# Attention with sinks on Trainium2: a reordering of the fourth unit's scores, the last queries' copies, the squares and the exponentials

## The chip, the cores and the metric

The kernel runs on one core of one Trainium2 chip. The metric is the device time of one execution in microseconds, lower is better; where a kernel was run several times, the median is given.

## The reference, cut to what matters

The program computes two transformer blocks of two layers each over 256 tokens of width 1024, in float32. The change lies in one step of the second block's second layer: attention with 16 query heads and 4 key heads of 64, a window of 128 keys, and a learned sink logit per head.

```python
def banded_sink_attention(q, k, v, sinks):
    ...
    logits = jnp.einsum('bnqhgd,bnkhd->bnhgqk', qb, kw) * (dh ** -0.5)
    ...
    logits = jnp.where(valid[None, :, None, None], logits, -jnp.inf)
    m = jnp.maximum(jnp.max(logits, axis=-1), sink)
    probs = jnp.exp(logits - m[..., None])
    denom = jnp.sum(probs, axis=-1) + jnp.exp(sink - m)
    out = jnp.einsum('bnhgqk,bnkhd->bnhgqd', probs, vw) / denom[..., None]

def swa_sink_mixer(h, positions, w_qkv, q_norm, k_norm, sinks, w_out):
    qkv = h @ w_qkv
    ...
    q = apply_rope_2(rms_norm_2(q, q_norm), cos, sin)
    k = apply_rope_2(rms_norm_2(k, k_norm), cos, sin)
    o = banded_sink_attention(q, k, v, sinks)
    return o.astype(h.dtype) @ w_out
```

## The kernel before, in words

**Weights.** Every weight matrix is loaded in pieces of 1 MB (queue of SyncE), and each piece is cut into two units. ScalarE copies a unit into a high part (`hi_to`, L383, about a microsecond), VectorE subtracts that from the raw data into a low part (`lo_to`, L391), and TensorE multiplies with three products for one (high by high, high by low, low by high). A unit's buffer comes free when TensorE is done with the unit six places before. `hi_to(main, n)` and `lo_to(main, n)` treat all units below n that are not yet treated. In this stage `U` is the first unit of the attention's weights: U to U+3 are the keys, U+4 to U+7 the first half of the queries, U+8 and U+9 the values, U+10 to U+13 the last queries, and U+14 to U+21 the output projection.

**The attention stage** runs from about 1940 to 2064 us. Each engine has its order written out by hand, in `pe_window`, `act_window` and `dve_window`, and semaphores join them. An engine works strictly down its own list: whatever stands behind a waiting instruction waits too. The steps are:

- `qk(n, c)` on TensorE projects a quarter of group n (2 the keys, 0 the first queries, 1 the last queries). Two quarters fill a bank of PSUM.
- `squares(n, i)` on ScalarE (L2467) squares a bank for the norm, `gained(n, i)` on VectorE (L2541) copies the same bank, times the norm's gain, into `QB`. It waits for the squares. These are the "copies" of the change's name.
- `sums(n)` on TensorE (L2318) sums the squares over each head with products that are 2 columns wide; it waits for both of the group's squares. `scales(n)` on VectorE (L2563 and the small operations behind it) makes the inverse roots.
- `rope(n)` on TensorE (L2326) rotates `QB`; `cosines(n)` and `sines(n)` on VectorE (L2546, L2552, L2556) finish the rotation.
- Scores come in eight units. Unit u belongs to key head u // 2 and to half u % 2 of the queries; the even ones see 128 keys, the odd ones 256. `logits(u)` on TensorE (L2363) makes them; `begin(u)` on VectorE is `masked(u)` (adds the mask, L2576 or L2579) and `maxima(u)` (L2589 to L2595; an even unit's `begin` takes the next even unit too). `soft(u)` on ScalarE (L2477, L2479) is the exponentials. `turned(u)` is the transposition on TensorE (L2378) and its copy out on ScalarE (L2485).
- `weigh(g, t)` on TensorE (L2393) multiplies by the values, `weighed(g, t)` on VectorE (L2608 to L2617) divides by the denominators, and `rows(g, t)` transposes the result back (L2402), and splits it into high and low parts (ScalarE L2489, VectorE L2625).
- `pe_project` multiplies by the output weights (L408 to L410), and does `logits(7)`, `turned(4)` and so on between its first four units.

"The fourth unit" of the change's name is unit 3. The values are copied out of PSUM by ScalarE at L2503, and `qk(1, 0)` needs the bank they leave. What the change touches are the lists in `pe_window` (L2427 to L2436), `act_window` (L2497 to L2520) and `dve_window` (L2652 to L2672).

Of the kernel before, what the change touches and what calls it, by code (L numbers as in the profile page):

```python
# [244 lines left out]
def program(nc, ctx, d, out, known, draft):  # L245
# [35 lines left out]
    main = Side(sig, "", all_loads(d), NS + NX)  # L281
# [34 lines left out]
    def bk(b):  # L316
        return PSM[:, b, :]
# [11 lines left out]
    def take(b):  # L329
        claim_bank(b)  # L330
        return bk(b)
# [43 lines left out]
    def hi_to(s, n, end=None):  # L375
        while s.hi_at < min(n, len(s.w.units) if end is None else end):
            i = s.hi_at
            m, h = s.w.units[i]
            if h == 0:
                A.wait_ge(*s.landed[s.w.loads[m][3]].of(m))  # L380
            if i >= NU:
                A.wait_ge(*s.pe.of(("unit", i - NU)))
            A.activation(unit(s, i)[0], raw_half(s, i), ACT.Copy).then_inc(*s.w_hi.tick(i))  # L383
            s.hi_at += 1

    def lo_to(s, n, end=None):
        while s.lo_at < min(n, len(s.w.units) if end is None else end):
            i = s.lo_at
            hi, lo = unit(s, i)
            V.wait_ge(*s.w_hi.of(i))  # L390
            V.tensor_tensor(lo, raw_half(s, i), hi.bitcast(F), SUB).then_inc(*s.w_lo.tick(i))  # L391
            s.lo_at += 1
# [1910 lines left out]
    def pe_window():  # L2303
# [9 lines left out]
        def sums(n):  # L2313
            ps = take(SS_BANK[n])
            T.wait_ge(*act.of(f"wi.sq{n}"))
            for t in range(2):
                for c in range(4):
                    x = T.matmul(ps[:, 8 * t + 2 * c:8 * t + 2 * c + 2], SQ[:, c, t * P:(t + 1) * P], C("bd2"), start=True, stop=True)  # L2318
            x.then_inc(*pe.tick(f"wi.ss{n}"))
            empties(SS_BANK[n], (dve, f"wi.ss{n}"))  # L2320
# [48 lines left out]
        def turned(u):  # L2369

            nb, banks, E = u % 2 + 1, PT_BANKS[u], WE[u % 4]
            for b in banks:
                take(b)
            T.wait_ge(*act.of(f"wi.e{u}"))
            for j in range(4):
                for kb in range(nb):
                    o = (j * nb + kb) * P
                    x = T.transpose(bk(banks[o // 512])[:, o % 512:o % 512 + P], E[:, j, kb * P:(kb + 1) * P], ident)  # L2378
            x.then_inc(*pe.tick(f"wi.T{u}"))
            for b in banks:  # L2380
                empties(b, (act, f"wi.pt{u}"))

        def weigh(g, t):

            b = AV_BANK[g][t]
            ps = take(b)
            T.wait_ge(*act.of("wi.v"))
            for i in range(2):
                u = 4 * g + 2 * i + t
                T.wait_ge(*act.of(f"wi.pt{u}"))  # L2390
                for j in range(4):
                    for kb in range(t + 1):
                        x = T.matmul(ps[:, 256 * i + 64 * j:256 * i + 64 * j + 64], WP[u % 4][:, j, kb * P:(kb + 1) * P],  # L2393
                                     WV[:, kb, (2 * g + i) * 64:(2 * g + i + 1) * 64], start=kb == 0, stop=kb == t)
            x.then_inc(*pe.tick(f"wi.av{g}{t}"))
            empties(b, (dve, f"wi.z{g}{t}"))
# [30 lines left out]
        turned(2)  # L2427
        qk(1, 3)
        turned(1)
        sums(1)  # L2430
        weigh(0, 0)
        rope(1)
        turned(3)
        weigh(0, 1)
        rows(0, 0)
        rows(0, 1)  # L2436
# [23 lines left out]
    def act_window():  # L2460
        U = un["wi.qk2a"][0]

        def squares(n, i):
            if n != 2:
                A.wait_ge(*pe.of(f"wi.ss{0 if n else 2}"))
            A.wait_ge(*pe.of(f"wi.qk{n}{i}"))
            A.activation(SQ[:, 2 * i:2 * i + 2, :], heads(bk(QK_BANKS[n][i]), 2), ACT.Square).then_inc(*act.tick(f"wi.sq{n}", f"wi.sq{n}{i}"))  # L2467

        def soft(u):
            nm, sm, sk, _ = soft_cols(u)  # L2470
            gr, t = u // 2, u % 2
            L = WE[u % 4]
            _, r, _, _ = win_scales(gr // 2)
            A.wait_ge(*dve.of(f"wi.m{u}"))
            for j in range(4):
                n = 8 * t + 4 * (gr % 2) + HEAD[j]
                A.activation(L[:, j, :], L[:, j, :], ACT.Exp, scale=r[:, n:n + 1], bias=nm[:, j:j + 1], accum_out=sm[:, j:j + 1]  # L2477
                             ).then_inc(*act.tick(f"wi.e{u}"))
            A.activation(sk, sk, ACT.Exp).then_inc(*act.tick(f"wi.e{u}"))  # L2479

        def turned(u):
            A.wait_ge(*pe.of(f"wi.T{u}"))
            w = 512 // (P * (u % 2 + 1))
            for i, b in enumerate(PT_BANKS[u]):
                A.activation(flat(WP[u % 4][:, w * i:w * i + w, :]), bk(b), ACT.Copy).then_inc(*act.tick(f"wi.pt{u}"))  # L2485

        def rows(g, t):
            A.wait_ge(*pe.of(f"wi.zT{g}{t}"))
            A.activation(XH[:, 4 * g:4 * g + 4, t * P:(t + 1) * P], heads(bk(WZ_BANK[g][t]), 4), ACT.Copy  # L2489
                         ).then_inc(*act.tick(f"wi.h{g}{t}"))  # L2490

        hi_to(main, U + 8)
        squares(2, 0)
        hi_to(main, U + 10)
        squares(2, 1)
        hi_to(main, U + 12)
        squares(0, 0)  # L2497
        hi_to(main, U + 14)
        squares(0, 1)
        hi_to(main, U + 16)  # L2500
        A.wait_ge(*pe.of("wi.v"))
        for t in range(2):
            A.activation(WV[:, t, :], bk(t)[:, 0:256], ACT.Copy, scale=RR[:, t:t + 1]).then_inc(*act.tick("wi.v"))  # L2503
        soft(0)
        soft(2)
        hi_to(main, U + 17)
        soft(1)
        squares(1, 0)
        turned(0)
        turned(2)  # L2510
        hi_to(main, U + 19)
        soft(3)
        squares(1, 1)
        turned(1)
        hi_to(main, U + 20)
        turned(3)
        rows(0, 0)
        rows(0, 1)
        soft(4)
        soft(6)  # L2520
        hi_to(main, U + 21)
        soft(5)
        turned(4)
        turned(6)
        hi_to(main, U + 22)
        soft(7)
        turned(5)
        hi_to(main, un["wi.o2"][0] + NU)
        turned(7)
        rows(1, 0)  # L2530
        rows(1, 1)

    def dve_window():
        U = un["wi.qk2a"][0]
        sn = S("sinks")

        def gained(n, i):
            if n != 2:
                V.wait_ge(*pe.of(f"wi.ro{0 if n else 2}"))
            V.wait_ge(*act.of(f"wi.sq{n}{i}"))  # L2540
            V.tensor_scalar(QB[:, 2 * i:2 * i + 2, :], heads(bk(QK_BANKS[n][i]), 2), S("akn") if n == 2 else S("aqn"), None, MUL  # L2541
                            ).then_inc(*dve.tick(f"wi.g{n}{i}"))
# [40 lines left out]
        def maxima(u):  # L2583
            nm, _, sk, x = soft_cols(u)
            gr, t, L = u // 2, u % 2, WE[u % 4]
            _, r, _, _ = win_scales(gr // 2)
            r4 = r[:, 8 * t + 4 * (gr % 2):8 * t + 4 * (gr % 2) + 4].rearrange("p (a b) -> p b a", a=2)
            V.wait_ge(*dve.of(f"wi.l{u}"))
            V.tensor_reduce(x, L, AX, MAX, negate=True).then_inc(*dve.tick())  # L2589
            V.wait_ge(*dve.last())  # L2590
            V.tensor_tensor(x.rearrange("p (b a) -> p b a", b=2), x.rearrange("p (b a) -> p b a", b=2), r4, MUL).then_inc(*dve.tick())
            V.wait_ge(*dve.last())
            V.tensor_tensor(nm, x, NSK[:, 4 * gr:4 * gr + 4], MIN).then_inc(*dve.tick())
            V.wait_ge(*dve.last())
            V.tensor_tensor(sk, nm, sn[:, 4 * gr:4 * gr + 4], ADD).then_inc(*dve.tick(f"wi.m{u}"))  # L2595

        def begin(u):
            masked(u)
            maxima(u)
            if u % 2 == 0:  # L2600
                maxima(u + 2)
# [20 lines left out]
        def rows(g, t):  # L2622
            V.wait_ge(*act.of(f"wi.h{g}{t}"))
            h = XH[:, 4 * g:4 * g + 4, t * P:(t + 1) * P]
            V.tensor_tensor(XL[:, 4 * g:4 * g + 4, t * P:(t + 1) * P], heads(bk(WZ_BANK[g][t]), 4), h.bitcast(F), SUB  # L2625
                            ).then_inc(*dve.tick(f"wi.x{g}{t}"))
# [25 lines left out]
        masked(1)  # L2652
        lo_to(main, U + 16)
        maxima(1)
        gained(1, 0)
        lo_to(main, U + 17)
        begin(3)
        lo_to(main, U + 18)
        gained(1, 1)
        cosines(1)  # L2660
        scales(1)
        weighed(0, 0)
        sines(1)
        lo_to(main, U + 19)
        weighed(0, 1)
        begin(4)
        rows(0, 0)
        rows(0, 1)
        masked(5)
        lo_to(main, U + 20)  # L2670
        maxima(5)
# [327 lines left out]
```

## Time and profile before

| | us |
|---|---|
| median of 3 runs | 2325.43 |
| lowest and highest | 2322.65, 2327.29 |
| the profiled execution's own time | 2323.32 |
| its span | 2321.5 |
| mean granted TensorE clock (share of full) | 0.962 |

The rows below come from the profiled execution, in microseconds from the start of its span. Busy time of TensorE is modelled and includes the pipeline, so the start of an instruction is the safer number. In a timeline a row shows the start, the duration, the engine, the line, the operation, what it writes and reads, how many, and in brackets the idle time of the engine before it and what ended that. The granted clock is given as a share of full: 1.00 is 2.4 GHz and 0.50 is 1.2 GHz.

### The profile page before, as it was taken

Reading aid. Unit: us, or ns where it says so; the run is one execution under the profiler, and the core shown is the slowest. Engines: PE = TensorE matmul, PEld = TensorE weight load, DVE = VectorE, ACT = ScalarE, POOL = GpSimd, SP = SyncE. Lnnn points to the kernel's source line nnn. Section 1 sums busy time; section 2 is a strip of 40 time slices with the busy share of each in tenths; the row PEclk is TensorE's granted clock in tenths of the full one; section 3 lists DMA queues with packets and bytes.
Section 4 is the critical chain, followed back from the end, with each engine's and each line's share of the span. In section 5 each row is a group of like instructions: output and inputs, shape, how many; then the busy total and the mean of one; then the engine's idle time right before and its main releaser. Section 6 shows DMA issues by size and latency. Waiting matters only on the chain.

```text
span 2321.5 us, 30709 instructions
## 1 busy us (share of the span) xinstructions
PE 2159.3 (93%) x12344; PEld 1892.9 (82%) x12344; DVE 1773.2 (76%) x2344; ACT 1394.2 (60%) x1845; POOL 45.1 (2%) x22
## 2 busy tenths in 40 slices
PE   7999999889999999999999999577789999789998
PEld 6889989778888888888888888366689988679996
DVE  4776666769999989899999999666676667666665
ACT  4544445558777777787777878444454454454444
POOL 0020001010000000000000000000000000000000
PEclk9999999989999999999999999788899999889999
DMA  8436544549999999999999999233245545135552
GB/s 281 141 129 207 193 139 153 208 174 379 349 377 357 359 351 356 356 361 364 345 371 350 368 339 371 85 113 105 91 161 184 182 133 180 55 100 191 182 180 97
DMA packets 280165, 546.62 MB, mean 235 GB/s; under 512 B 8524, under 2 KB 113616, under 8 KB 279888
## 3 DMA queue, kind: packets, MB, share of 16 engines
q1 hardware_dynamic: 276800, 535.33, 65.9%
q10 hardware_dynamic: 3040, 8.72, 1.1%
q8 instruction: 100, 1.64, 0.3%
q0 software_dynamic: 176, 0.53, 0.1%
q14 instruction: 49, 0.40, 0.1%
HBM read 543.49 MB, written 1.05 MB: 235 GB/s over the span
## 4 chain that ended last, share of the span: by engine, by line
PE 87%; DVE 8%; ACT 3%; DMA 1%; issue 1%; DVEq 0%; SPq 0%; ACTq 0%
PE psum L408 19%; PE psum L410 18%; PE psum L409 18%; PE psum L402 8%; PE psum L403 8%; PE psum L404 8%; DVE wl L391 2%; PE psum L1689 1%; PE psum L1709 1%; DMA raw<-in_w_in 1%; PE psum L1699 1%; ACT XT L444 1%; PE psum L2393 1%; DVE arena L2137 0%; PE psum L437 0%
## 5 line engine op out<-in xcount | busy, mean ns | idle before, releaser
L391 DVE TENSOR_TENSOR wl<-raw,wh 128x1024 fp32r<-128x1024 f32 x640 | 771.6, 1229 | 201.9 <-ACT wh L383 196.8
L383 ACT ACTIVATE wh<-raw 128x1024 fp32r<-128x1024 f32 x640 | 662.8, 1050 | 319.2 <-PE psum L404 149.6
L402 PE MATMUL psum<-xh,wh 128*128 128x256 f32 x1600 | 464.2, 290 | 26.6 <-DVE wl L391 18.9
L391 DVE TENSOR_TENSOR wl<-arena,wh 128x1024 fp32r<-128x1024 f32 x384 | 458.0, 1221 | 32.4 <-ACT wh L383 23.6
L408 PE MATMUL psum<-wh,xh 128*128 128x512 f32 (+1 forms) x1152 | 457.6, 397 | 19.9 <-DVE xl L428 10.4
L383 ACT ACTIVATE wh<-arena 128x1024 fp32r<-128x1024 f32 x384 | 404.5, 1062 | 94.5 <-PE psum L410 94.5
L403 PE MATMUL psum<-xl,wh 128*128 128x256 f32 x1600 | 460.4, 288 | 0.0
L404 PE MATMUL psum<-xh,wl 128*128 128x256 f32 x1600 | 459.9, 287 | 0.0
L410 PE MATMUL psum<-wh,xl 128*128 128x512 f32 (+1 forms) x1152 | 451.1, 392 | 0.0
L409 PE MATMUL psum<-wl,xh 128*128 128x512 f32 (+1 forms) x1152 | 450.9, 391 | 0.0
L402 PEld LDWEIGHTS psum<-xh,wh 128*128 128x128 f32 x1600 | 314.8, 197 | 33.8 <-DVE wl L391 14.5
L403 PEld LDWEIGHTS psum<-xl,wh 128*128 128x128 f32 x1600 | 315.1, 197 | 1.6 <-issue 0.5
L404 PEld LDWEIGHTS psum<-xh,wl 128*128 128x128 f32 x1600 | 314.7, 197 | 0.0
L408 PE MATMUL psum<-wh,yh 128*128 128x512 f32 x736 | 288.5, 392 | 2.4 <-DVE yl L1837 1.4
L409 PE MATMUL psum<-wl,yh 128*128 128x512 f32 x736 | 287.0, 390 | 0.0
L410 PE MATMUL psum<-wh,yl 128*128 128x512 f32 x736 | 286.7, 390 | 0.0
L408 PEld LDWEIGHTS psum<-wh,xh 128*128 128x128 f32 x1152 | 218.9, 190 | 66.3 <-DVE xl L428 10.6
L410 PEld LDWEIGHTS psum<-wh,xl 128*128 128x128 f32 x1152 | 218.6, 190 | 46.1
L409 PEld LDWEIGHTS psum<-wl,xh 128*128 128x128 f32 x1152 | 219.1, 190 | 43.3
L408 PEld LDWEIGHTS psum<-wh,yh 128*128 128x128 f32 x736 | 138.4, 188 | 30.3 <-DVE yl L1837 1.6
L410 PEld LDWEIGHTS psum<-wh,yl 128*128 128x128 f32 x736 | 138.2, 188 | 29.0
L409 PEld LDWEIGHTS psum<-wl,yh 128*128 128x128 f32 x736 | 138.4, 188 | 26.9
(362 smaller groups left out, 1633.2 us busy)
## 6 DMA issues: line engine op xcount, KB each, us to landing
arena<-in_moe_g SPq DMA_DIRECT2D x72, 1024.0 KB, 7.3
arena<-in_moe_u SPq DMA_DIRECT2D x72, 1024.0 KB, 7.8
raw<-in_moe_d SPq DMA_DIRECT2D x64, 1024.0 KB, 7.5
arena<-in_moe_d SPq DMA_DIRECT2D x48, 1024.0 KB, 6.9
raw<-in_ff_up SPq DMA_DIRECT2D x48, 1024.0 KB, 5.2
raw<-in_moe_g SPq DMA_DIRECT2D x40, 1024.0 KB, 7.5
raw<-in_moe_u SPq DMA_DIRECT2D x40, 1024.0 KB, 7.4
raw<-in_ff_down SPq DMA_DIRECT2D x24, 1024.0 KB, 5.0
```

The costliest lines, as they stand in the source:

```text
L383: A.activation(unit(s, i)[0], raw_half(s, i), ACT.Copy).then_inc(*s.w_hi.tick(i))
L391: V.tensor_tensor(lo, raw_half(s, i), hi.bitcast(F), SUB).then_inc(*s.w_lo.tick(i))
L402: T.matmul(ps, wh, x[0][:, k, :], start=k == 0, stop=False)
L403: T.matmul(ps, wh, x[1][:, k, :], start=False, stop=False)
L404: i = T.matmul(ps, wl, x[0][:, k, :], start=False, stop=k == kn - 1)
L408: T.matmul(ps, x[0], w[0], start=first, stop=False)
L409: T.matmul(ps, x[0], w[1], start=False, stop=False)
L410: return T.matmul(ps, x[1], w[0], start=False, stop=last)
L444: A.activation(o, i, ACT.Copy, scale=sc).then_inc(*act.tick(f"{st}.k{t}"))
L1689: i = T.matmul(MB[:, k * CAP:(k + 1) * CAP], X[:, t, (4 * b + k) * P:(4 * b + k + 1) * P], SE[:, t, :], start=t == 0, stop=t == 1)
L1699: i = T.matmul(MB, ST[e % 2][:, t * P:(t + 1) * P], YE[z][:, h * 512:(h + 1) * 512], start=z == 0, stop=z == 1)
L1709: i = T.transpose(TB[:, c * P:(c + 1) * P], HT[k][:, c * P:(c + 1) * P], ident)
```

## The change

Only the order of steps in three lists changes; every instruction and every wait of its own stays. On TensorE, `weigh(0, 0)` and `turned(3)` go ahead of `sums(1)` and `rope(1)`. On ScalarE, the copies of the values go ahead of the conversion of unit U+15; `squares(1, 1)` goes ahead of `soft(3)`; unit U+18 is converted behind `turned(1)` and not ahead of `soft(3)`, and U+19 behind `turned(3)`. On VectorE, `begin(3)` goes ahead of unit U+16 and of `gained(1, 0)`; `gained(1, 1)` goes ahead of unit U+17; unit U+18 goes behind `weighed(0, 1)`, and `begin(4)` behind both `rows`.

```diff
--- before.py
+++ after.py
@@ -2427,10 +2427,10 @@
         turned(2)
         qk(1, 3)
         turned(1)
+        weigh(0, 0)
+        turned(3)
         sums(1)
-        weigh(0, 0)
         rope(1)
-        turned(3)
         weigh(0, 1)
         rows(0, 0)
         rows(0, 1)
@@ -2497,10 +2497,10 @@
         squares(0, 0)
         hi_to(main, U + 14)
         squares(0, 1)
-        hi_to(main, U + 16)
         A.wait_ge(*pe.of("wi.v"))
         for t in range(2):
             A.activation(WV[:, t, :], bk(t)[:, 0:256], ACT.Copy, scale=RR[:, t:t + 1]).then_inc(*act.tick("wi.v"))
+        hi_to(main, U + 16)
         soft(0)
         soft(2)
         hi_to(main, U + 17)
@@ -2508,12 +2508,13 @@
         squares(1, 0)
         turned(0)
         turned(2)
+        hi_to(main, U + 18)
+        squares(1, 1)
+        soft(3)
+        turned(1)
         hi_to(main, U + 19)
-        soft(3)
-        squares(1, 1)
-        turned(1)
+        turned(3)
         hi_to(main, U + 20)
-        turned(3)
         rows(0, 0)
         rows(0, 1)
         soft(4)
@@ -2652,20 +2653,20 @@
         masked(1)
         lo_to(main, U + 16)
         maxima(1)
+        begin(3)
+        lo_to(main, U + 17)
         gained(1, 0)
-        lo_to(main, U + 17)
-        begin(3)
+        gained(1, 1)
         lo_to(main, U + 18)
-        gained(1, 1)
         cosines(1)
         scales(1)
         weighed(0, 0)
         sines(1)
+        weighed(0, 1)
         lo_to(main, U + 19)
-        weighed(0, 1)
-        begin(4)
         rows(0, 0)
         rows(0, 1)
+        begin(4)
         masked(5)
         lo_to(main, U + 20)
         maxima(5)
```

## Rows read from the trace of the kernel before

**Rows 1.** The page, part 1: busy time of each engine over the whole span.
```profile
PE 2159.3 (93%) x12344; PEld 1892.9 (82%) x12344; DVE 1773.2 (76%) x2344; ACT 1394.2 (60%) x1845; POOL 45.1 (2%) x22
```

**Rows 2.** Waits, 1940 to 2100 us: line waited for, us in total, times, longest.
```profile
PE psum L2318 <- ACT arena L2467: 6.5, 1, 6.5
...
PE psum L408 <- DVE xl L2625: 4.3, 1, 4.3
...
PE psum L402 <- ACT arena L2503: 1.9, 1, 1.9
```

**Rows 3.** Timeline of ScalarE, 1968 to 2062 us: start, length, line, idle before.
```profile
1980.16 1.06 ACT L383 ACTIVATE wh<-raw 128x1024 fp32r<-128x1024 f32 x1 [5.25 <-PE psum L410]
1981.12 0.82 ACT L2503 ACTIVATE arena<-psum,SC 128x256 f32<-128x256 f32 x2
```

**Rows 4.** Stretches: length, busy us of each engine, granted clock, DMA share, GB/s.
```profile
1980.10:1982.00 1.90, 0.03 (x2) 0.01 (x1) 1.76 (x6) 1.82 (x4) 0.00 (x0) 1.00 0.02 6
1982.50:1985.80 3.30, 3.30 (x17) 3.30 (x17) 0.00 (x0) 0.74 (x1) 0.00 (x0) 0.50 0.00 0
2003.10:2007.00 3.90, 0.01 (x1) 0.04 (x1) 1.77 (x6) 3.18 (x11) 0.00 (x0) 0.50 0.22 59
2016.80:2025.20 8.40, 7.83 (x73) 6.91 (x71) 5.66 (x12) 2.28 (x4) 0.00 (x0) 1.00 0.00 0
2030.40:2033.50 3.10, 3.10 (x9) 2.42 (x8) 2.94 (x6) 0.77 (x5) 0.00 (x0) 0.50 0.16 36
2051.95:2052.92 0.97, 0.00 (x0) 0.01 (x1) 0.89 (x3) 0.00 (x0) 0.00 (x0) 1.00 1.08 385
```

**Rows 5.** Timeline of ScalarE, later part of the same stretch.
```profile
1999.62 2.00 ACT L383 ACTIVATE wh<-raw 128x1024 fp32r<-128x1024 f32 x2
2003.82 0.60 ACT L2477 ACTIVATE arena<-arena,SC 128x256 f32<-128x256 f32 x1 [2.21 <-DVE SC L2595]
...
2006.27 0.57 ACT L2467 ACTIVATE arena<-psum 128x512 f32<-128x512 f32 x1
```

**Rows 6.** Timeline of VectorE, 1968 to 2062 us: start, length, line, idle before.
```profile
1998.87 0.75 DVE L2541 TENSOR_SCALAR arena<-psum,smalls 128x512 f32<-128x512 f32 x1 [3.17 <-ACT arena L2467]
...
2000.67 1.28 DVE L2576 TENSOR_TENSOR arena<-psum,consts 128x512 f32<-128x512 f32 x2
...
2010.57 0.36 DVE L2563 TENSOR_SCALAR SC<-psum,SC 128x8 f32<-128x8 f32 x2 [1.61 <-PE psum L2318]
...
2013.22 0.15 DVE L2608 TENSOR_TENSOR SC<-SC 128x4 f32<-128x4 f32 x1
...
2014.15 0.75 DVE L2617 TENSOR_TENSOR arena<-psum,SC 128x256 f32<-128x256 f32 x2 [0.30 <-PE psum L2393]
2017.19 1.29 DVE L2552 TENSOR_TENSOR arena<-psum,CS 128x512 f32<-128x512 f32 x2 [2.28 <-PE psum L2326]
...
2019.66 1.22 DVE L391 TENSOR_TENSOR wl<-raw,wh 128x1024 fp32r<-128x1024 f32 x1
...
2028.11 1.28 DVE L2625 TENSOR_TENSOR xl<-psum,xh 128x512 fp32r<-128x512 f32 x2
```

**Rows 7.** Chain that ended last, 1940 to 2100 us: start, length, line.
```profile
1973.75 1.72 PE psum L2326 x4
1975.47 1.68 PE psum L2318 x16
...
2006.99 3.54 PE psum L2318 x16
...
2018.03 3.52 PE psum L2393 x32
...
2022.56 0.63 PE psum L2402 x4
...
2041.69 1.73 PE psum L2393 x16
...
2047.07 0.87 PE psum L2378 x8
```

## The prediction

> **What bounds the kernel now.** First the page: TensorE is busy for 93% of the span [rows 1], so a microsecond of its idle time, or of its low clock, is a microsecond of the whole wherever the next stage follows without slack. The change touches one stage of some 120 us, so I read the waits of TensorE in that stage next [rows 2]. There are three that matter: 6.5 us in which `sums(1)` waits for ScalarE's squares, 4.3 us in which the output projection waits for VectorE's low part, and 1.9 us in which `qk(1, 0)` waits for ScalarE's copy of the values. Then the timelines of ScalarE and VectorE for why they are late, and last the granted clock, because each wait has an echo. The clock was 1.00 during the wait of 1.9 us and 0.50 in the 3.3 us read behind it; it was 0.50 late in the long wait, and again behind the 4.3 us; behind a wait of 0.97 us it stayed at 1.00 [rows 4].
>
> *The long wait.* VectorE ended the maxima of unit 1 at 1998.87 - 3.17 = 1995.70 and then stood 3.17 us for the first square [rows 6]. Only then came U+16 and `begin(3)`, which started at 2000.67. So the exponentials of unit 3 could start only at 2003.82, after ScalarE had itself stood 2.21 us [rows 5]. `squares(1, 1)` is behind them in ScalarE's list and started at 2006.27, though its input had been ready since TensorE left `qk(1, 3)`, before 1999.7. `sums(1)` started at 2006.99. It is a circle: VectorE waits for ScalarE, then ScalarE for VectorE, then TensorE for both.
>
> **The change part by part,** against the profiled execution (2323.32 us, span 2321.5; the median of the runs is 2.1 us above it).
>
> (a) *The values' copies ahead of U+15.* Conversion and copies start at 1980.16 and 1981.12 [rows 3], so the copies come 0.96 us earlier and so does TensorE. **-0.95 us.** U+15 comes 0.8 us later; its low part isn't wanted before VectorE has done units 0 and 1's scores, which wait for TensorE themselves. Free; without that cover it would cost 0.8.
>
> (b) *The echo of that wait.* The clock was 0.50 for some 3.4 us after it, which is 1.7 us lost. The wait left is 0.95 us. Bounds: 0 (the clock falls all the same, as behind 1.9 us) and -1.7 (it doesn't, as behind 0.97 us) [rows 4]. The nearest row is the second: **-1.7 us.** From here everything runs 2.65 us earlier.
>
> (c) *From `turned(1)` to the start of the last `rows(0, 1)` on TensorE.* Before: the hole begins at 2006.99 - 6.5 = 2000.5, `turned` takes 0.87 [rows 7], so `turned(1)` starts at 1999.6; `rows(0, 1)` starts at 2022.56. That is 22.9 us. After, with the shift, `turned(1)` starts at 1996.95. VectorE has the maxima of unit 1 at 1993.05 and goes straight on: `begin(3)` took from 2000.67 to 2003.8, so they are there at 1996.2. ScalarE reaches its conversion of U+17 at 1999.62 - 2.65 = 1996.97, does one unit instead of two (1.0 us, half of 2.00), then `squares(1, 1)` (0.5) until 1998.45, then `soft(3)`, which took 2003.82 to 2006.27 = 2.45 us, until 2000.9 [rows 5].
>
> TensorE at full clock: `turned(1)` to 1997.8, `weigh(0, 0)` (1.73, the same step at full clock [rows 7]) to 1999.55, a **new wait** for unit 3's exponentials to 2000.9 (1.35 us; the sums, the rotation and everything after stand behind it), `turned(3)` to 2001.8, sums (1.68) to 2003.5, rotation (1.72) to 2005.2, `weigh(0, 1)` (3.52) to 2008.7. The sums took 3.54 at the low clock before [rows 7].
>
> VectorE decides the end, though. Behind the sums it does scales (2010.57 to 2013.22: 2.65), `weighed(0, 0)` (to 2014.90, 0.30 of it a wait: 1.4), sines (2017.19 to 2019.66: 2.5) and `weighed(0, 1)` (1.3) [rows 6], together 7.85. So `rows(0, 1)` starts at 2003.5 + 7.85 = 2011.4. That is 14.4 us where there were 22.9: a gain of 8.5 at full clock. TensorE then has a second new wait, some 2 us ahead of `rows(0, 1)`.
>
> The clock is the unknown. This stretch now has two short waits, and between them products only 2 and 64 columns wide. Fast bound: it stays up, as it did from 2016.8 to 2025.2 in just such narrow work with 0.57 us idle [rows 4]: -8.5. Slow bound: it falls in the new wait and stays low through `turned(3)` and the sums (+2.6 until the sums are done) and most of the rotation, up again within `weigh(0, 1)`: the projection's row starts some 3.3 us later, -5.2. I take a fall of ordinary length, +1.9: **-6.6 us.**
>
> (One rule of the Trainium skill speaks against the change here. "TensorE: Matmul & The Clock Gate", Part 4: PE-mode transpose, says that transposes don't count as TensorE's activity, so `turned(3)` would not hold the clock up. By it alone the slow bound would be the value, 1.4 us less gain. The trace shows the clock at 1.00 across a stretch with `turned` in it, but it can't show those alone.)
>
> (d) *Behind it.* Before, `rows(0, 1)` at 2022.56 to `turned(7)` at 2047.07 is 24.5 us [rows 7]. In it stand the wait of 4.3 us, there because VectorE did `begin(4)`, with two units' maxima, ahead of `rows` at 2028.11 [rows 6], and 3.4 us at 0.50 behind it, 1.7 lost [rows 4]. Now VectorE does U+18 (1.2) and the two `rows` (1.28) first: the low parts are there 2.5 us after `rows(0, 1)` starts, and TensorE is busy with `logits(4)` and `logits(5)` until then. The wait goes, -4.3, and its echo, -1.7. Against that, `begin(4)`, the exponentials of 4 and 6 and then of 5 come later by the two `rows` and U+18: by the same durations ScalarE has the copies for `weigh(1, 0)` 13.9 us after `rows(0, 1)` starts, TensorE could start it after 12.8: +1.1. And the clock may still fall once in the narrow stretch: +0.9 as the middle of 0 and 1.7. **-4.0 us**, bounds -2.5 and -6.0. From `turned(7)` on all is as before, only earlier. SyncE's loads are released by low parts: the next feed-forward's first one comes some 4 us earlier, into an idle queue. Nothing.
>
> Sum: 0.95 + 1.7 + 6.6 + 4.0 = 13.25. From 2323.3 that is 2310.1; from the median, 2325.4, it is **2312**. All high: 0.95 + 1.7 + 8.5 + 6.0 = 17.2, 2308. All low: 0.95 + 0 + 5.2 + 2.5 = 8.7, 2317. The runs before spread by 2.3 us about their middle, which gives 2306 to 2319.
>
> **The rivals.**
>
> *B, the gain behind the projection's start is given back.* VectorE and ScalarE need as long for units 4 to 7 as before, so `weigh(1, 0)` and `turned(7)` wait and (d) is nothing: 2325.4 - 9.2 = 2316. For it: the two engines' lists there have little slack. Against: ScalarE stands idle for 9 us around `turned(3)` before, none of which it needs. 0.12.
>
> *C, the clock stays at half from the new wait into the projection.* The rotation and the weighing take double: `rows(0, 1)` starts at about 2017.3, 5.3 earlier than before rather than 11.2, and the first two projection units lose 2.7 of what (d) wins: about 2320. For it: the long stretch at 0.50 before, from 2003.1 to 2016.5, had the same narrow sums in it. Against: the clock rose in the rotation there. 0.10.
>
> *D, slower.* The same mechanism without end. From `turned(3)` (2000.9) to `turned(7)` TensorE has 26.2 us of work at full clock: 10.9 in four projection units, 15.3 in the steps between. All of it at half is 52.4, so `turned(7)` at 2053.3 instead of 2047.1: 2331. It becomes slower from the point at which some 21 of the 26 us run at half. Against: behind the 4.3 us wait the clock was back after 3.4 us of wide products [rows 4]. 0.03.
>
> *E, the change doesn't do what it says.* ScalarE comes to `squares(1, 1)` at 1998.0, TensorE leaves `qk(1, 3)` at 1996.9. That is 1.1 us of slack. If the values' products or `qk` end later than I have it, ScalarE stands at the squares with unit 3's exponentials, both `turned` copies and so `weigh(0, 1)` behind it; the hole moves in place of closing, and what remains is (a), (b) and a little: 2322. 0.05.
>
> **How the numbers follow.** The forecast has 0.70, B 0.12, C 0.10, E 0.05, D 0.03. The time is the forecast's, 2312. The range takes in its own 2306 to 2319, B, and most of C: 2306.5 to 2320. About 0.2% (4.7 us, so a limit of 2320.8) is what a measurement of this kernel can tell from no change. Faster by more: forecast, B and two thirds of C, 0.88. Within: the rest of C and most of E, 0.08. Slower: D and a remainder, 0.04.
>
> **What would show it.** In the waits of TensorE, L2318 <- L2467 (6.5) gone and a wait of L2378 for L2477 of 1 to 1.5 us in its place; L402 <- L2503 down to 0.9 with the clock at 1.00 behind it; L408 <- L2625 gone or under 0.5; L2402 <- L2617 up to some 2 us. VectorE's 3.17 us ahead of L2541 gone, a wait for the sums in its place. `rows(0, 1)` near 2013 and `turned(7)` near 2034. I am wrong if TensorE's wait for L2477 is over 3 us (then E), if L2393 waits for L2485 by more than 2 us (B), or if the clock is 0.50 over more than 7 us after `turned(3)` (C, D).

## The result, and the profile after

The changed kernel takes 2317.89 us in the median of its first nine runs (2309.31 to 2321.19), the kernel before 2326.48 (nine runs, 2322.65 to 2328.82). The ratio is 0.995, interval 0.9936 to 0.9965: 8.6 us less in the medians, where 13.4 were forecast, and inside the range. A second set of six runs gave 2310.15 and a ratio of 0.9943 (0.9922 to 0.9964); over all fifteen the median is 2312.0. The fifteen fall into two groups, eight at 2308.8 to 2312.0 and seven at 2317.9 to 2321.2, with nothing between; the median of the nine lies in the upper one, because five of the nine do. The first profile, at 2321.17 us, is of the upper group; a second one, at 2311.39 us, is of the lower.

The page of the first profile, part 1, answers to [rows 1]; TensorE is as busy as before, in modelled time that a low clock stretches:

```profile
PE 2164.9 (93%) x12344; PEld 1896.2 (82%) x12344; DVE 1771.7 (76%) x2344; ACT 1393.9 (60%) x1845; POOL 45.1 (2%) x22
```

The waits of TensorE in the stage, 1940 to 2100 us, answer to [rows 2] (us in total, times, longest):

```profile
PE psum L2378 <- ACT SC L2479: 1.5, 1, 1.5
...
PE psum L2402 <- DVE arena L2618: 1.2, 2, 1.0
...
PE psum L402 <- ACT arena L2502: 0.9, 1, 0.9
```

The wait of 6.5 us for the squares and the one of 4.3 us for VectorE's low part are gone. In their place stands a wait of `turned(3)` for unit 3's exponentials, 1.5 us, and the one for the values' copies is halved. (Lines behind the change are one higher: L2502 is L2503 before.)

ScalarE's timeline answers to [rows 3] and [rows 5]; a row shows start, length, line and idle time before. The values' copies come first, and the exponentials of unit 3 follow the square without a gap:

```profile
1986.28 0.84 ACT L2502 ACTIVATE arena<-psum,SC 128x256 f32<-128x256 f32 x2 [9.79 <-PE psum L410]
1987.01 2.00 ACT L383 ACTIVATE wh<-raw 128x1024 fp32r<-128x1024 f32 x2
...
2004.25 0.58 ACT L2467 ACTIVATE arena<-psum 128x512 f32<-128x512 f32 x1
2004.72 0.60 ACT L2477 ACTIVATE arena<-arena,SC 128x256 f32<-128x256 f32 x1
```

So far it is the forecast. The granted clock is not (stretches as in [rows 4]; the clock is the third number from the end):

```profile
1987.20:2007.30 20.10, 18.72 (x160) 17.62 (x160) 15.79 (x29) 16.05 (x46) 0.00 (x0) 1.00 0.17 54
2008.00:2028.20 20.20, 20.04 (x89) 16.83 (x87) 11.02 (x35) 4.27 (x7) 0.00 (x0) 0.50 0.16 52
2028.40:2060.00 31.60, 30.56 (x177) 25.99 (x177) 20.40 (x51) 18.55 (x52) 0.00 (x0) 1.00 0.32 101
```

It fell 0.4 us behind the new wait, in `turned(3)`, and stayed at 0.50 for 20.5 us, through the sums, the rotation, `weigh(0, 1)`, both `rows` and the scores behind them; it came back at 2028.3, just ahead of the output projection's first product. The chain that ended last (start, length, line), which answers to [rows 7], shows what that cost:

```profile
2003.32 0.89 PE psum L2378 x8
...
2007.41 1.55 PE psum L2378 x8
2008.96 3.21 PE psum L2318 x16
2012.17 3.62 PE psum L2326 x4
2015.79 6.73 PE psum L2393 x32
...
2023.52 1.08 PE psum L2402 x4
...
2044.42 0.87 PE psum L2378 x8
```

The sums took 3.21 us, the rotation 3.62 and `weigh(0, 1)` 6.73, which is 3.52 at full clock. Now the same rows of the profile of the lower group, the same kernel:

```profile
1999.38 0.89 PE psum L2378 x8
...
2003.47 1.06 PE psum L2378 x8
2004.54 2.87 PE psum L2318 x16
2007.40 3.62 PE psum L2326 x4
2011.03 3.87 PE psum L2393 x32
...
2015.89 0.63 PE psum L2402 x4
...
2034.65 0.87 PE psum L2378 x8
```

```profile
2004.90:2011.60 6.70, 6.70 (x21) 4.63 (x21) 3.67 (x21) 2.24 (x4) 0.00 (x0) 0.50 0.38 130
2011.80:2040.00 28.20, 27.11 (x192) 23.37 (x191) 22.84 (x51) 17.59 (x49) 0.00 (x0) 1.00 0.28 93
```

Here the clock fell 1.3 us behind the new wait, was at 0.50 for 6.8 us only, and came back in `weigh(0, 1)`.

The three profiles can be set side by side by the starts of a few steps, in us from the stage's first product (`qk(2, 0)`; taken from TensorE's timeline; the last column is the first product of the next feed-forward):

| kernel | turned(1) | rows(0, 1) | turned(7) | stage ends | clock at 0.50 in between |
|---|---|---|---|---|---|
| before | 59.7 | 82.8 | 107.1 | 135.0 | 3.4 + 13.7 + 3.4 |
| after, 2321.17 us | 56.3 | 76.6 | 97.4 | 125.3 | 20.5 |
| after again, 2311.39 us | 57.0 | 73.6 | 92.2 | 120.2 | 6.8 |

In between leaves out the low clock at the stage's start and end, which every kernel has. The stage is 9.8 us shorter in the one and 14.9 in the other. The 5.1 us between the two are only half of what lies between these profiles of the same kernel: their spans differ by 9.8 us, 5.1 of it in this stage and 4.6 ahead of it, in code that the change doesn't touch (the stage began at 1946.90 and at 1942.26 us). The profile before had it at 1939.80, which is why the two spans compared, 2321.5 and 2319.4, hide most of the stage's gain.

### The profile page after: what moved, and what is told of

Same layout as the page of the kernel before. It is cut to its first block, busy times and chain, and to the rows that moved or that the text cites. A ratio compares the mean times of both kernels' runs of the same rounds, so it can differ in the third digit from the quotient of the medians.

```text
span 2319.4 us, 30709 instructions
## 1 busy us (share of the span) xinstructions
PE 2164.9 (93%) x12344; PEld 1896.2 (82%) x12344; DVE 1771.7 (76%) x2344; ACT 1393.9 (60%) x1845; POOL 45.1 (2%) x22
## 4 chain that ended last, share of the span: by engine, by line
PE 87%; DVE 8%; ACT 2%; DMA 1%; issue 1%; DVEq 0%; SPq 0%; ACTq 0%
PE psum L408 19%; PE psum L410 18%; PE psum L409 18%; PE psum L402 8%; PE psum L403 8%; PE psum L404 8%; DVE wl L391 1%; PE psum L1689 1%; PE psum L1709 1%; DMA raw<-in_w_in 1%; PE psum L1699 1%; ACT XT L444 1%; PE psum L2393 1%; PE psum L437 1%; DVE arena L2137 0%
```

## The experiments

### Each part alone, on the kernel before

**e1: the values' copies first.**

```diff
-        hi_to(main, U + 16)
         A.wait_ge(*pe.of("wi.v"))
...
+        hi_to(main, U + 16)
         soft(0)
```

> Part (a) alone on the kernel before: the values' copies ahead of the conversion of U+15. Theory 1 (the wait has an echo in the clock): the wait of qk(1, 0) goes from 1.9 to 0.95 us and the clock behind it stays at 1.00, so 2.6 us less where the clock fell before, and 1 to 2.5 us in the median. Theory 2 (the echo is chance, it was absent in the changed kernel because of where the clock's own fall came): only the 0.95 us, which a median hardly shows. The circle behind it is untouched: sums(1) still waits 6 to 7 us for the squares.

Measured: 2327.0 us against 2328.12, ratio 0.9992 (0.9982 to 1.0002), not to be told from none. In the profile the wait is 0.93 us and the clock stayed at 1.00 in it and in the 21.7 us behind it; `sums(1)` started at 64.7 us of the stage and not 67.2. Then the 2.5 us were lost again. The clock, low since the wait for the squares, came up at the same 76.8 us of the stage as before, so more of the work ran at half, and `rows(0, 1)` was only 1.3 us earlier. And it fell within the projection's wait and not behind it, for 6.8 us where it was 3.4, so the stage ended at 134.7, 0.3 us earlier.

```profile
1984.00:1984.85 0.85, 0.00 (x0) 0.00 (x0) 0.70 (x5) 0.84 (x3) 0.00 (x0) 1.00 0.11 43
1985.00:2006.70 21.70, 16.93 (x144) 15.73 (x144) 14.65 (x27) 15.43 (x41) 0.00 (x0) 1.00 0.15 49
2030.80:2037.40 6.60, 5.31 (x12) 3.80 (x12) 5.13 (x9) 2.96 (x14) 0.00 (x0) 0.50 0.27 83
```

So the part does what (a) and (b) say, and the stage can give it back at its next waits. The echo isn't always there with a wait of 1.9 us: e3 and e12 below both have that wait. In e3 the clock fell behind it, in e12 it did not:

```profile
1987.65:1989.45 1.80, 0.00 (x0) 0.00 (x0) 1.67 (x5) 1.78 (x3) 0.00 (x0) 1.00 0.03 11
1990.00:1993.20 3.20, 3.20 (x17) 3.20 (x17) 0.00 (x0) 0.74 (x1) 0.00 (x0) 0.50 0.00 0
```

```profile
1982.95:1984.75 1.80, 0.00 (x0) 0.00 (x0) 1.66 (x6) 1.77 (x3) 0.00 (x0) 1.00 0.04 14
1985.00:2007.70 22.70, 21.23 (x185) 20.16 (x184) 15.21 (x28) 16.79 (x49) 0.00 (x0) 1.00 0.23 75
```

Of the four profiles with 1.9 us (before, e2, e3, e12) two have the echo; of the ten with 0.93 us none. It goes with the start of the stage: where the clock had come up at 5.1 us of it (before, e3) it fell behind the 1.9 us, where at 2.9 (e2, e12) it didn't. Five of the ten with 0.93 us had it up at 5.1 us too (e1, e4, e8, e9, e11), and in none did it fall there; with the start alike, the shorter wait removed the echo.

**e2: the middle alone.** The changed kernel with the values' copies (e1's diff the other way round) and VectorE's rows as before, of which this is the edit:

```diff
-        weighed(0, 1)
         lo_to(main, U + 19)
-        rows(0, 0)
-        rows(0, 1)
+        weighed(0, 1)
         begin(4)
+        rows(0, 0)
+        rows(0, 1)
```

> The middle part alone: TensorE's, ScalarE's and VectorE's new order around squares(1, 1) and begin(3), with the values' copies and the two rows of VectorE where they were. Theory 1 (the gain of the stage is the circle that is broken, 9.75 us in the two profiles): 5 to 8.5 us faster, depending on whether the clock falls in the new wait; the output projection still waits 4 us for VectorE's low part. Theory 2 (most of the gain is that projection's wait): 2 us or less.

Measured: 2323.72 us against 2328.12, ratio 0.998 (0.9969 to 0.9991): 4.4 us, just under theory 1's 5 to 8.5 and above theory 2's 2 or less, though the interval reaches down to 2.1. Its profile was its fastest run (2319.35, the others reach 2327.87); the stage took 128.1 there, 7.0 less, so the profile flatters it. The projection's wait was still 3.4 us:

```profile
PE psum L408 <- DVE xl L2626: 3.4, 1, 3.4
...
PE psum L2378 <- ACT SC L2479: 1.5, 1, 1.5
```

**e3: VectorE's rows first, alone.** The same lines the other way round, on the kernel before.

> Part (d) alone: VectorE does U+18 and both rows ahead of begin(4), everything else as before. Theory 1: the wait of 4.3 us ahead of the output projection goes and its echo in the clock too; ScalarE's later copies give about 1 us back: 3.5 to 5 us faster. Theory 2 (rival B, the gain is given back by the scores of units 4 to 7): 0 to 1.5 us, with TensorE waiting at weigh(1, 0) or turned(7) instead.

Measured: 2322.8 us against 2328.12, ratio 0.9983 (0.9973 to 0.9993). The stage took 130.7, 4.4 less; the projection didn't wait. Theory 1; rival B is out. Up to `turned(7)` the gain was 5.8 us; the clock gave 1.4 of it back, for here it fell 0.1 us behind the last wait of 1.0 us, that of `rows(1, 1)`, behind which it had stayed up before:

```profile
2053.70:2054.70 1.00, 0.04 (x1) 0.07 (x2) 0.95 (x3) 0.00 (x0) 0.00 (x0) 1.00 1.09 383
2054.85:2058.10 3.25, 3.25 (x11) 2.67 (x10) 0.95 (x2) 0.60 (x1) 0.00 (x0) 0.50 0.25 85
```

The same happened in e2; in the other twelve profiles it didn't.

### Each part taken from the changed kernel

**e12: the values' copies back.** e1's diff the other way round.

> The changed kernel without part (a): U+15 ahead of the values' copies, as before. Theory 1 (the wait of 1.9 us and its echo in the clock): 1 to 2.6 us slower than the changed kernel. Theory 2 (the wait alone): 0.95 us slower, which the median doesn't show clearly; in the profile the wait of qk(1, 0) is 1.9 us.

Measured: 2313.48 us, ratio to before 0.9943 (0.9931 to 0.9956). That is the changed kernel's own ratio in its second set: part (a) is worth nothing here that five runs show, although the wait is 1.9 us again (the first stretch of e12 above). Theory 1 and its 1 to 2.6 us aren't seen; theory 2 forecast that 0.95 us wouldn't show. The stage took 118.8 us in the profile, 1.4 less than in the better one of the changed kernel, for the clock was low for 3.4 us only.

**e11: VectorE's rows back.** e2's diff alone.

> The changed kernel without part (d): begin(4) ahead of both rows on VectorE, as before. Theory 1 (the parts add): 4 to 5 us slower than the changed kernel, as (d) alone on the kernel before gave, with the projection's wait of 3.4 to 4.3 us back. Theory 2 (the parts overlap, for the earlier low parts meet a later ScalarE): 0 to 2 us slower.

Measured: 2322.31 us, ratio to before 0.9984 (0.9972 to 0.9996). The changed kernel stood at 2312.0 and 0.9943 to 0.995, so this is 8 to 10 us slower: more than the 4 to 5 of theory 1, and more than e3 gave. e2 and e12 differ by the same part, and by 0.0037 in the ratio, 8.6 us. So the parts seem to do more together than alone; the intervals are just wide enough that a plain sum isn't excluded. The projection's wait was back in full,

```profile
PE psum L408 <- DVE xl L2626: 4.3, 1, 4.3
```

and the clock was low twice, for 6.8 us each, in a stage of 127.6 us.

**e10: unit U+18 ahead of the exponentials again.** This undoes the move of one conversion on ScalarE, and lengthens the new wait.

```diff
         squares(1, 1)
+        hi_to(main, U + 19)
         soft(3)
         turned(1)
-        hi_to(main, U + 19)
```

> The changed kernel with one piece undone: ScalarE converts U+18 ahead of soft(3) again, so the exponentials, and with them the new wait of turned(3), come 1.0 us later: 1.5 becomes 2.5 us. Theory 1 (the new wait is paid in full, and in clock): 1 to 3 us slower than the changed kernel in the median, stage 121.5 us and more. Theory 2 (VectorE bounds this stretch, TensorE has slack of about 0.6 us): 0.5 us slower, or nothing.

Measured: 2317.71 us (2312.03 to 2321.96), ratio to before 0.9957 (0.9943 to 0.9971); the median is 5.7 us above the changed kernel's 2312.0, but the ratio only 0.07 to 0.14% above its two, with intervals that overlap. So a slower median isn't shown clear of noise. The profile has the wait at 2.4 us, and the clock low for 20.5 us, as in the upper group:

```profile
PE psum L2378 <- ACT SC L2479: 2.4, 1, 2.4
```

```profile
2004.90:2025.20 20.30, 20.15 (x90) 16.95 (x88) 11.00 (x35) 3.54 (x6) 0.00 (x0) 0.50 0.12 43
```

Against the second profile of the changed kernel, where the clock's steps lie at the same places up to the wait (up at 4.5 and 4.6 us of the stage, down at 62.5 and 62.6), the stage took 127.0 and not 120.2: 6.8 us more beside 0.9 us more of wait, most of it in the clock. That is one profile against one, and the changed kernel itself had both lengths of low clock with the same wait, so the 6.8 us aren't shown to be the price of the 0.9.

### The new wait and the clock

**The changed kernel again.**

> The changed kernel once more, unchanged. Its first nine runs fell into two groups, 2309 to 2312 and 2318 to 2321 us. Theory 1 (the groups are how long the clock is low behind the new wait): a profile of 2309 to 2312 us has the clock at 0.50 for 3.4 to 10 us between turned(3) and the projection, one of 2318 to 2321 has it for some 20 us, and the stage takes 120 to 122 us in the first and 125 in the second. Theory 2 (the groups come from the stages ahead of this one): the stage takes 125 us in both, and the difference stands at the start of the stage.

Measured: above. Both theories hold by half: the low clock was 6.8 us and the stage 120.2, as theory 1 has it, and the other half of the difference stood at the stage's start.

**e6 and e7: the wait filled.** Ahead of `turned(3)`:

```diff
         weigh(0, 0)
+        T.matmul(take(5), C("rot"), C("sel4"), start=True, stop=True)
         turned(3)
```

```diff
         weigh(0, 0)
+        fill = take(5)
+        for j in range(8):
+            T.transpose(fill[:, j % 4 * P:(j % 4 + 1) * P], C("rot"), ident)
         turned(3)
```

> The changed kernel with one product of constants, 512 columns wide (0.86 us of TensorE), put into its wait for unit 3's exponentials; its result is not used, the computation is complete. Theory 1 (the clock falls because the array has too little to do around the wait): the wait shrinks from 1.5 to 0.6 us, nothing is later, the clock falls less often or comes back sooner, and the median is 1 to 5 us below the changed kernel. Theory 2 (the filler is only work): no change, or up to 0.5 us slower.

> The same, but the filler is eight transpositions of a constant (0.87 us of TensorE too); the computation is complete. Theory 1 (a transposition holds the clock as well as a wide product): the same median as with the wide filler, within 1.5 us. Theory 2 (transpositions don't count as activity, as the Trainium skill's TensorE: Matmul & The Clock Gate says in Part 4: PE-mode transpose): as the changed kernel, with the wide filler 1 to 5 us ahead.

Measured: 2310.1 us (0.9939, 0.9923 to 0.9954) with the wide filler and 2311.92 (0.9941, 0.9927 to 0.9955) with transpositions. Neither can be told from the changed kernel or from the other. The profiles say more, for in both the clock came up where it did in the second profile of the changed kernel, at 4.5 to 4.6 us of the stage. With either filler the wait shrank from 1.5 to 0.6 us, and the clock stayed at 1.00 over the wait, the sums and the rotation, for 11.5 us from `turned(3)` on, where it had been at 0.50 without one. First the wide filler, then the transpositions:

```profile
2001.00:2012.50 11.50, 9.20 (x70) 7.90 (x71) 8.64 (x31) 4.30 (x7) 0.00 (x0) 1.00 0.28 93
2012.70:2015.90 3.20, 3.20 (x24) 2.75 (x22) 2.68 (x6) 0.40 (x1) 0.00 (x0) 0.50 0.00 0
```

```profile
2001.00:2012.50 11.50, 9.19 (x70) 7.89 (x70) 8.64 (x31) 4.31 (x7) 0.00 (x0) 1.00 0.29 93
2012.70:2015.90 3.20, 3.20 (x24) 2.77 (x22) 2.67 (x6) 0.41 (x1) 0.00 (x0) 0.50 0.00 0
```

The other profiles bear this out. Those with the new wait, in the order of how soon the clock fell behind its end:

| kernel | wait | clock falls behind its end after | and is low for |
|---|---|---|---|
| after | 1.48 | 0.4 | 20.5 |
| e10 | 2.41 | 0.4 | 20.5 |
| e5, after again | 1.49 | 1.3 | 6.8 |
| e11 | 1.46 | 1.6 | 6.8 |
| e2 | 1.48 | 2.9 | 3.4 |
| e12 | 1.47 | 2.9 | 3.4 |

In all six it fell within 3 us of the wait; in the five that had work in its place (e6, e7 and, below, e4, e8, e9) it stayed up until the wait at `rows(0, 1)`, or (e9) to the stage's end. So the unfilled wait brought the fall, and the sooner the fall, the longer it lasted; why, no run shows. The filler brought no time all the same: TensorE came to `rows(0, 1)` earlier, waited 2.3 us there for VectorE where it had waited 0.6, and the clock fell behind that; with the wide filler,

```profile
PE psum L2402 <- DVE arena L2619: 3.3, 2, 2.3
```

The stage took 120.1 in both. (The Trainium skill, "TensorE: Matmul & The Clock Gate", Part 4: PE-mode transpose, says that transpositions don't count as activity. The traces don't agree here: eight of them held the clock as one wide product did, 1.00 over the same 11.5 us. That is one profile each.)

**e4: the sums and the rotation ahead of `turned(3)`.**

```diff
         weigh(0, 0)
-        turned(3)
         sums(1)
         rope(1)
+        turned(3)
         weigh(0, 1)
```

> The changed kernel with sums(1) and rope(1) put ahead of turned(3) on TensorE: the wait of 1.5 us for unit 3's exponentials is filled with the sums, and VectorE's scales can start 2 us earlier. Theory 1 (the new wait and the idle array behind it cost time and clock): the wait goes, the clock falls less often, 2 to 6 us faster than the changed kernel, so 11 to 14 us faster than before. Theory 2 (the clock falls in this stretch because of the narrow products, not because of the wait): 1.5 us faster than the changed kernel, and the clock is at 0.50 for 10 us or more in the profile all the same.

**e8: only the sums.** `sums(1)`, `turned(3)`, `rope(1)`.

> The changed kernel with only sums(1) put ahead of turned(3), rope(1) behind it: the two changes of the faster order taken apart. Theory 1 (what counts is that the sums fill the wait for the exponentials and that VectorE's scales start earlier): all of the gain of that order, 5 to 7 us below the changed kernel, and no wait of turned(3) for ScalarE over 0.3 us. Theory 2 (the rotation, with its wide products, has to come early too, to hold the clock): 2 to 4 us below the changed kernel only, and the clock falls in the profile behind the sums.

Measured: e4 2311.02 us, ratio to before 0.9929 (0.9912 to 0.9946), and e8 2312.13, 0.993 (0.9913 to 0.9947). The stage took 117.9 and 118.0, with one low stretch of 3.4 us each. In the profiles that is theory 1 twice: the sums fill the wait, `rows(0, 1)` starts at 69.9 us of the stage, and the rotation's place doesn't matter. In time neither theory's gain over the changed kernel is shown: against the changed kernel of the same set e8's ratio is 0.1% lower, inside the intervals, and its median 2.0 us higher. Where `turned(3)` stands is thus a part of the change that seems to win nothing: e4's order on TensorE differs from that of the kernel before only in that `weigh(0, 0)` is ahead of `sums(1)`, and its stage is the shorter by 2 to 7 us. What both still had was TensorE's wait at `rows(0, 1)`; in e4:

```profile
PE psum L2402 <- DVE arena L2618: 2.6, 2, 1.6
```

**e9: the scores of units 4 and 6 into that wait.** On top of e4:

```diff
         rows(0, 0)
-        rows(0, 1)
         logits(4)
+        rows(0, 1)
         logits(5)
```

> The order with sums(1) and rope(1) ahead of turned(3), and logits(4) besides put between rows(0, 0) and rows(0, 1), where TensorE still waited 1.55 us for VectorE. Theory 1: the 1.2 us of logits(4) fill that wait, which falls under 0.5 us, VectorE finds unit 4's scores ready, and the stage takes 116 to 117 us where it took 117.9. Theory 2 (VectorE and ScalarE bound the stretch behind it): the wait turns up again at weigh(1, 0) or at the output projection, and the stage stays at 117.5 to 118. In the median 1 us is not to be told from none.

Measured: 2308.67 us against 2326.9, ratio 0.9926 (0.9913 to 0.9938), the lowest of the study. The stage took 116.5. The wait of 1.55 us gave way to three small ones (the 1.0 us one is at the later `rows(1, 1)`, as in every kernel), and between the stage's start and its end the clock never fell:

```profile
PE psum L2402 <- DVE arena L2618: 1.0, 1, 1.0
...
PE psum L408 <- DVE xl L2626: 0.6, 1, 0.6
...
PE psum L2363 <- DVE SC L2609: 0.3, 1, 0.3
...
PE psum L2393 <- ACT arena L2485: 0.2, 1, 0.2
```

```profile
1945.00:2050.00 105.00, 98.62 (x731) 87.78 (x730) 79.15 (x186) 56.70 (x134) 0.00 (x0) 1.00 0.34 111
```

It beats the kernel before by 0.7%. Against the changed kernel it is lower in the medians and its five runs (2305.4 to 2312.5) have none in the upper group; the interval of its ratio overlaps with those of both sets of the changed kernel.

## Why the prediction was right, and where not

**(a) Right in the profile, not in the median.** The copies came first and the wait went from 1.87 to 0.93 us in each of the ten profiles that have the new order. e12 shows no cost when it is undone.

**(b) Right for the profile it was read from, too large as a mean.** The profile before had the echo, but two of the four profiles with that wait don't. "The nearest row" was the right choice for the wait that is left (0.93 us never had an echo); the error was to take the echo of 1.87 us as certain. From the stage's start to `turned(1)` it was 2.7 and 3.4 us less in the two profiles, forecast 2.65, of which part is where the clock came up at the stage's start; in e1 and e11, where it came up as in the profile before, it was 2.4 us. The forecast leaned on the wait of 0.97 us [rows 4] behind which the clock stayed up. That row shows only the wait itself, and in e3 and e2 the clock fell behind that same wait (1.0 us by TensorE's timeline), though behind the values' 0.93 us it never did.

**(c) The term that was mis-sized: its slow bound.** `turned(1)` to `rows(0, 1)` took 23.1 us before, 16.7 in the second profile after and 20.4 in the first: gains of 6.4 and 2.7, where the forecast took 6.6 with bounds of 8.5 and 5.2. The new wait was 1.48 us (forecast 1.35), the steps on VectorE were as priced: scales 2.66, `weighed(0, 0)` 1.34, sines 2.45 in the second profile. The bound assumed that the clock would come up again within `weigh(0, 1)`, as it had come up in the rotation before. It did so in the second profile. In the first and in e10 it did not, and the clock stayed at half through `weigh(0, 1)`, both `rows` and the scores. With that the path changed too. The forecast had VectorE decide when `rows(0, 1)` starts; in the first profile VectorE stood 3.3 us for TensorE's `weigh(0, 1)`:

```profile
2022.62 0.76 DVE L2618 TENSOR_TENSOR arena<-psum,SC 128x256 f32<-128x256 f32 x2 [3.34 <-PE psum L2393]
```

Where the clock held (e6, e7) VectorE did decide, with TensorE waiting 2.3 us (forecast some 2), and `turned(1)` to `rows(0, 1)` took 15.0 us where the fast bound had 14.4. One reading was wrong besides: the products between the two waits are not only 2 and 64 columns wide, the rotation's four are 512. That first profile is rival C, given one in ten at about 2320 (its own terms, 5.3 and 4.0 less 2.7, come to 2319), and the sign for it, a clock at 0.50 for more than 7 us behind `turned(3)`, was there. Seven of fifteen runs came in at 2317.9 to 2321.2, near its time, and the one that was profiled took its path; that the other six did too was not seen.

**(d) Between its bounds.** `rows(0, 1)` to `turned(7)` went from 24.3 to 18.6 us in the second profile, and to 20.7 in the first, with the clock low at its start: 5.8 and 3.6, forecast 4.0 with bounds of 6.0 and 2.5. Most of the 1.1 us that ScalarE was to give back didn't come: in the second profile `weigh(1, 0)` started 13.3 us after `rows(0, 1)`, with TensorE there after 13.3 (forecast 12.8) and the copies done after 13.5 (forecast 13.9). e3 had the sign and the size without the rest: 5.8 us up to `turned(7)`, 4.4 of the stage. Behind `turned(7)` the stage took 27.9 us in all three profiles, as said.

Sum over the stage: 14.9 us in the second profile and 9.8 in the first; the forecast was 13.25. Both are between its bounds of 8.7 and 17.2. The one number that the rest hung on was how often C comes. That the forecast time of 2312 is also the median of all fifteen runs is luck: it is the upper edge of the lower group, and the sum stands for a fall of middle length, between the two that were seen. The range took in both groups but for the three highest runs.

B is out by e3 and by the profiles (no wait of L2393 for L2485 over 0.3 us). D is out: the longest low clock ended 20.5 us after it fell, ahead of the projection, and the slowest of fifteen runs took 2321.2. E is out: the square followed the conversion without a gap.

**Left open:** why the clock comes up soon behind the same rotation in one execution and not in another. The two differ in when the clock came up at the stage's start (2.9 and 4.5 us of it), but e2 and e12 have the first's 2.9 and only 3.4 us of low clock behind the new wait, and no run sets it by itself. Which of the middle part's moves breaks the circle was not taken apart; e2 has them all. Also open is why the stages ahead of this one took 4.6 us longer in the first profile.

## What to carry to other kernels

When two engines wait for each other in turn and the third for both, look for the operation whose input has long been there and which only stands behind a waiting one; moving that one forward breaks the circle without shortening any step. A wait on TensorE should be priced with the clock that may fall behind it: here the same wait of 1.5 us was followed by 3.4 to 20.5 us at half clock, half of which is lost where TensorE is what the stage waits for, so one profile gives one draw of the price and not its mean. Filling the wait with work whose inputs are ready (the sums, then the scores) kept the clock up and gave the shortest stages, 118 and 116.5 us. And a change that removes several waits has to be measured whole, since each part alone can be given back at the next wait.

## What the runs showed of the hardware

- The same binary took 6.8 us or 20.5 us at half clock in the same stretch, and its fifteen runs fell into two groups 6 us apart.
- With a wait of 1.87 us the clock fell in two profiles of four; with 0.93 us at the same place in none of ten; with 1.0 us at `rows(1, 1)` in two of fourteen.
- Behind an unfilled wait of about 1.5 or 2.4 us it fell in six profiles of six, after 0.4 to 2.9 us, and stayed low for 3.4, 6.8 or 20.5 us, the longer the sooner it fell. With work in that place it fell there in none of five.
- Eight transpositions of 0.87 us in all kept the clock up as one product 512 columns wide and 0.86 us long did.
